# Two transformer blocks on one Trainium2 core: the start is reordered, and three visits of four modulation slabs move to layer boundaries

## Reference

```python
# first block, for layer L in 0, 1
h = rms_norm(x, norm_w[L])
q, k, v, z, q_h, f_h, i_h, g_h, gate_a, gate_h = split(h @ w_in[L])
a = window_attention(rope(q, positions), rope(k, positions), v, sinks[L]) * silu(z)
b = norm(hgrn2(silu(q_h), f_h, i_h)) * silu(g_h)      # gated linear recurrence
x = x + (sigmoid(gate_a) * (a @ w_up_attn[L]) + sigmoid(gate_h) * (b @ w_up_hgrn[L])) @ w_out[L]
x = rms_norm(x, final_norm_w)
# second block, for layer i in 0, 1
mod = silu(c) @ ada_w[i] + ada_b[i]                   # ada_w[i] is 1024 x 6144; 6 vectors of 1024
sh_t, sc_t, g_t, sh_c, sc_c, g_c = split(mod, 6)
y = mixer_i(x * (1 + sc_t) + sh_t, rel_bias)          # i = 0: top-k latent attention; i = 1: differential
x = layer_norm(alpha * x + (1 + g_t) * y)
y = square(relu((x * (1 + sc_c) + sh_c) @ w1[i])) @ w2[i]
x = layer_norm(alpha * x + (1 + g_c) * y)
```

## Time and profile before

| | us |
|---|---|
| three executions without the profiler | 1336.64, 1339.19, 1339.91 (median 1339.19) |
| the profiled execution, its own time | 1346.1 |
| its span, first to last instruction | 1344.0 |
| PE busy in it | 1131.1 (84%) |
| POOL, ACT, DVE busy | 743.7, 550.8, 483.0 |
| mean granted clock of TensorE | 0.893 |

### The profile page before, as it was taken

The page is one execution under the profiler, slowest core; times in us unless marked ns, Lnnn a source line. Parts: engine busy times, 40 slices in busy tenths (PEclk is TensorE's granted clock), DMA queues, the critical chain, the costliest instruction groups (busy, mean ns, idle before and its releaser), DMA issues.

```text
span 1344.0 us, 15901 instructions
## 1 busy us (share of the span) xinstructions
PE 1131.1 (84%) x6584; PEld 954.6 (71%) x6584; DVE 483.0 (36%) x689; ACT 550.8 (41%) x749; POOL 743.7 (55%) x341
## 2 busy tenths in 40 slices
PE   2789698787796988879889699999698657999995
PEld 0778576656685766669678698888687446899894
DVE  3426633232457152323752511113600564301114
ACT  2455354323544363344442344344224432444441
POOL 1475362744464554646204487778457206588883
PEclk9899899897897988989857899999799668899997
DMA  7365333745461535475302366775287203456550
GB/s 282 119 248 190 128 124 114 243 176 178 177 238 65 188 105 208 147 245 157 126 0 66 99 230 231 278 261 180 92 302 272 88 0 126 153 181 195 175 174 32
DMA packets 101022, 221.58 MB, mean 165 GB/s; under 512 B 11360, under 2 KB 17878, under 8 KB 94806
## 3 DMA queue, kind: packets, MB, share of 16 engines
q1 hardware_dynamic: 95776, 210.29, 45.9%
q10 hardware_dynamic: 5174, 10.28, 2.1%
HBM read 219.48 MB, written 1.07 MB: 164 GB/s over the span
## 4 chain that ended last, share of the span: by engine, by line
PE 67%; DVE 14%; ACT 7%; DMA 4%; issue 3%; POOL 3%; ACTq 1%; POOLq 0%; DVEq 0%; SPq 0%
PE lin_ps L321 12%; PE lin_ps L322 11%; PE lin_ps L323 11%; PE tmp_ps L328 5%; PE tmp_ps L330 5%; PE tmp_ps L329 5%; PE tmp_ps L376 3%; PE lin_ps L328 3%; POOL wlo L805 3%; PE tmp_ps L419 2%; PE lin_ps L329 2%; PE lin_ps L330 2%; PE tmp_ps L516 2%; DMA ring<-in_b_w_in 2%; ACT whi L880 2%
## 5 line engine op out<-in xcount | busy, mean ns | idle before, releaser
L805 POOL TENSOR_TENSOR wlo<-ring,whi 128x1024 fp32r<-128x1024 f32 (+2 forms) x304 | 724.6, 2396 | 484.3 <-ACT whi L880 483.3
L880 ACT CAST whi<-ring 128x1024 fp32r<-128x1024 f32 (+2 forms) x304 | 312.6, 1035 | 534.2 <-PE lin_ps L323 244.2
L321 PE MATMUL lin_ps<-whi,hThi 128*128 128x512 f32 (+2 forms) x528 | 212.3, 402 | 27.2 <-POOL wlo L805 12.1
L322 PE MATMUL lin_ps<-wlo,hThi 128*128 128x512 f32 (+2 forms) x528 | 206.3, 391 | 0.0
L323 PE MATMUL lin_ps<-whi,hTlo 128*128 128x512 f32 (+2 forms) x528 | 205.9, 390 | 0.0
L328 PE MATMUL tmp_ps<-hThi,whi 128*128 128x256 f32 x520 | 149.5, 287 | 4.9 <-DVE hTlo L1517 4.9
L330 PE MATMUL tmp_ps<-hThi,wlo 128*128 128x256 f32 x520 | 148.7, 286 | 0.0
L329 PE MATMUL tmp_ps<-hTlo,whi 128*128 128x256 f32 x520 | 148.7, 286 | 0.0
L321 PEld LDWEIGHTS lin_ps<-whi,hThi 128*128 128x128 f32 x528 | 103.4, 196 | 60.1 <-issue 20.8
L328 PE MATMUL lin_ps<-hThi,whi 128*128 128x256 f32 x352 | 106.8, 303 | 30.2 <-POOL wlo L805 18.1
L323 PEld LDWEIGHTS lin_ps<-whi,hTlo 128*128 128x128 f32 x528 | 102.8, 195 | 20.8
(11 more groups left out here) (246 smaller groups left out, 1514.2 us busy)
## 6 DMA issues: line engine op xcount, KB each, us to landing
ring<-in_mlp_w SPq DMA_DIRECT2D x64, 1024.0 KB, 5.3
ring<-in_ada_w SPq DMA_DIRECT2D x48, 1024.0 KB, 5.5
ring<-in_w_in SPq DMA_DIRECT2D x40, 1024.0 KB, 5.3
ring<-in_b_w_in SPq DMA_DIRECT2D x12, 1024.0 KB, 5.7
ring<-in_w_out SPq DMA_DIRECT2D x8, 1024.0 KB, 5.2
ring<-in_a_w_in SPq DMA_DIRECT2D x6, 1024.0 KB, 5.8
ring<-in_w_up_hgrn SPq DMA_DIRECT2D x4, 1024.0 KB, 6.1
ring<-in_w_up_attn SPq DMA_DIRECT2D x4, 1024.0 KB, 9.8
```

The lines of the kernel that those rows point to most:

```text
L321: pe.matmul(ps, xh, hi, start=first, stop=False, skip_group_check=True)
L322: pe.matmul(ps, xh, lo, start=False, stop=False, skip_group_check=True)
L805: pool.tensor_tensor(wlo[:, n % PARTS, :, 0:width], ring[:, u % RING, 2 * h:2 * h + 2, 0:width], whi[:, n % PARTS, :, 0:width].bitcast(F32 ...
L880: act.copy(whi[:, n % PARTS, :, 0:width], ring[:, u % RING, 2 * h:2 * h + 2, 0:width]).then_inc(S("high_formed"), 1)
```

## The change

Nothing is computed otherwise; the order changes.

- **Start.** Layer 0 of the first block has no visit before its first product. On ACT, the squares of x come right after the issue of the transfers, then the first three highs, and only then what needs `cols`. On DVE the scaling of x comes first, then `cols`, the turned operand's low part, and after it the angles, `lbw` and `lams`. PE does `relvec` after the `kv` product, before the visit there. `csil`, the two bias loads (`gate_bias`, 512 KB each) and the Sin stand on ACT behind the Silu of `qh`. SP waits for x before it loads the second weight block. `posi` has a semaphore of its own. POOL waits for the scaled x before it forms the first lows (`f_scaled`, in both layers).
- **Visits.** The visits of 4 at the start of layer 0 and before `aT` in both layers go. Visits of 4 come at the boundaries `s0`, `s1` and `s2`, on PE before the wait for x, on DVE after the scaled x. Layer 1's visit of 4 stays. So group 0 fills at the end of layer 0 (and closes there, without the spread row), group 1 at layer 1's level 6, group 2 at `s0`, where it is closed after `s0iq`.

The diff, cut to its core (the long DVE block is moved as it is):

```diff
+ADA_BOUNDARIES = ("s0", "s1", "s2")
...
-            pe.wait_ge(S("small_landed"), 16 * 10)
+            pe.wait_ge(S("small_landed"), 16 * 9)
             ps = open_tmp("cols")
             pe.transpose(ps[:, 0, 0:P], stackA[:], ident[:])
             close_tmp(pe.transpose(ps[:, 0, P:P + 5 + 8 * KT], stackB[:], ident[0:5 + 8 * KT, 0:5 + 8 * KT]), "cols")
-            ps = open_tmp("relvec")
-            pe.wait_ge(S("rel_landed"), 32)
-            close_tmp(pe.matmul(ps[0:16, 0, 0:DIST], relT[:], onehot[:], start=True, stop=True), "relvec")
             quads_a = [(i, g) for i in range(NT) for g in range(2)]
             for L in range(2):
                 w = I["w_in"][L]
-                if L == 0:
-                    pe.wait_ge(S("csil"), 1)
-                ada(4)
+                if L:
+                    ada(4)
                 pe.wait_ge(S("f_scaled"), L + 1)
                 feature_major(f"f{L}hT", hs)
...
                 linear_tok(f"f{L}kv", w, K0, 256, hT)
+                if L == 0:
+                    ps = open_tmp("relvec")
+                    pe.wait_ge(S("rel_landed"), 32)
+                    close_tmp(pe.matmul(ps[0:16, 0, 0:DIST], relT[:], onehot[:], start=True, stop=True), "relvec")
+                    pe.wait_ge(S("csil"), 1)
...
-                ada(4)
                 pe.wait_ge(S("f_a"), L + 1)
...
+                if name in ADA_BOUNDARIES:
+                    ada(4)
...
+            ada_close()
...
+                if n == 1:
+                    sp.wait_ge(S("x_landed"), 16)
                 if n >= RING:
...
             row, one = st[:, 1, :, 0], st[:, 2, :, 0]
             rstd("f0", row, one)
+            pool.wait_ge(S("f_scaled"), 1)
             rstd("f0h", st[:, 1], st[:, 2], "f0ho")
             rstd("f1", row, one, "f0out1")
+            pool.wait_ge(S("f_scaled"), 2)
             rstd("f1h", st[:, 1], st[:, 2], "f1ho")
...
             act.dma_start(posi[:], I["positions"].rearrange("b (i p) -> p (b i)", p=P),
-                          allow_slow_non_contiguous=True).then_inc(S("small_landed"), 16)
+                          allow_slow_non_contiguous=True).then_inc(S("posi_landed"), 16)
...
-            act.wait_ge(*read_of("cols"))
-            act.activation(csil[:], colA[:, 120:128].unsqueeze(2).broadcast_to([P, KT, ADA_ROWS]), ACT.Silu
-                           ).then_inc(S("csil"), 1)
-            act.wait_ge(S("angles"), 1)
-            act.activation(trig[:], ang[:], ACT.Sin).then_inc(S("trig"), 1)
-            act.wait_ge(S("lb_max"), 1)
-            act.activation(lbw[:, 0:2, :], lbw[:, 0:2, :], ACT.Exp).then_inc(S("lb_exp"), 1)
-            act.wait_ge(S("lam_dots"), 1)
-            act.activation(lams[:, 0:2], lams[:, 0:2], ACT.Exp).then_inc(S("lam_exp"), 1)
-            act.wait_ge(*read_of("relvec"))
-            act.dma_start(scratch, relvec).then_inc(S("scratch_written"), 16)
                 if L == 0:
-                    for j in range(2):
-                        gate_bias(0, j)
                     squares("f0", (S("x_landed"), 16))
+                    high_parts(PARTS, 0)
+                    act.wait_ge(*read_of("cols"))
...
+                if L == 0:
+                    act.wait_ge(S("lb_max"), 1)
+                    act.activation(lbw[:, 0:2, :], lbw[:, 0:2, :], ACT.Exp).then_inc(S("lb_exp"), 1)
+                    act.wait_ge(S("lam_dots"), 1)
+                    act.activation(lams[:, 0:2], lams[:, 0:2], ACT.Exp).then_inc(S("lam_exp"), 1)
                 ahead(f"f{L}f")
...
                 read(act.activation(flat(qin), flat(ps), ACT.Silu), f"f{L}qh")
+                if L == 0:
+                    act.activation(csil[:], colA[:, 120:128].unsqueeze(2).broadcast_to([P, KT, ADA_ROWS]), ACT.Silu
+                                   ).then_inc(S("csil"), 1)
+                    for j in range(2):
+                        gate_bias(0, j)
+                    act.wait_ge(S("angles"), 1)
+                    act.activation(trig[:], ang[:], ACT.Sin).then_inc(S("trig"), 1)
...
                 read(act.mul(qkv[:, :, 0:HALF], ps, HD ** -0.5), f"f{L}q")
+                if L == 0:
+                    act.wait_ge(*read_of("relvec"))
+                    act.dma_start(scratch, relvec).then_inc(S("scratch_written"), 16)
...
-            ps = full_tmp_of(dve, "cols")
-            dve.tensor_copy(colA[:], ps[:, 0, 0:P])
-            read(dve.tensor_copy(colB[:], ps[:, 0, P:P + 5 + 8 * KT]), "cols")
-            ps = full_tmp_of(dve, "relvec")
-            read(dve.tensor_copy(relvec, ps[0:16, 0, 0:DIST]), "relvec")
-            dve.wait_ge(S("small_landed"), 16 * 10)
...
-                ada()
+                if L:
+                    ada()
+                else:
+                    ps = full_tmp_of(dve, "cols")
+                    dve.tensor_copy(colA[:], ps[:, 0, 0:P])
+                    read(dve.tensor_copy(colB[:], ps[:, 0, P:P + 5 + 8 * KT]), "cols")
                 for h in range(2):
...
+                if L == 0:
+                    dve.wait_ge(S("posi_landed"), 16)
+                    dve.wait_ge(S("invf"), 1)
+                    step(dve.tensor_copy(posf[:], posi[:]))
+                    for i in range(NT):
...
+                if L == 0:
+                    ps = full_tmp_of(dve, "relvec")
+                    read(dve.tensor_copy(relvec, ps[0:16, 0, 0:DIST]), "relvec")
                 ada()
...
-                ada()
                 low_of(f"f{L}aT0", 0)
...
+            ada()
...
+                if after in ADA_BOUNDARIES:
+                    ada()
                 if n == 3:
...
+            ada_close()
```

More of the change, by code:

```diff
@@ L1180, in _ @@
                               ).then_inc(S("levels_both"), 1)
-            ps = full_tmp_of(dve, "cols")
-            dve.tensor_copy(colA[:], ps[:, 0, 0:P])
-            read(dve.tensor_copy(colB[:], ps[:, 0, P:P + 5 + 8 * KT]), "cols")
-            ps = full_tmp_of(dve, "relvec")
-            read(dve.tensor_copy(relvec, ps[0:16, 0, 0:DIST]), "relvec")
-            dve.wait_ge(S("small_landed"), 16 * 10)
-            dve.wait_ge(S("invf"), 1)
-            step(dve.tensor_copy(posf[:], posi[:]))
@@ L1191, in _ @@
-            for i in range(NT):
-                for c in range(2):
-                    ins = dve.tensor_scalar(ang[:, i, c, :], invf[:], posf[:, i:i + 1], None, ALU.mult)
-            step(ins)
-            for c in range(2):
-                ins = dve.tensor_scalar(angk[:, :, c, :], ang[:, :, c, :], 1.0 / TURN, 0.25 * c, ALU.mult, ALU.add)
-            step(ins)
-            step(dve.tensor_scalar(angk[:], angk[:], ROUNDER, None, ALU.add))
-            step(dve.tensor_scalar(angk[:], angk[:], -ROUNDER, None, ALU.add))
@@ L1200, in _ @@
-            for part in TURN_PARTS:
-                step(dve.scalar_tensor_tensor(ang[:], angk[:], -part, ang[:], ALU.mult, ALU.add))
-            step(dve.tensor_scalar(ang[:, :, 1, :], ang[:, :, 1, :], TURN / 4, None, ALU.add))
-            dve.tensor_scalar(ang[:], ang[:], SIN_MAX, -SIN_MAX, ALU.min, ALU.max).then_inc(S("angles"), 1)
-            step(dve.tensor_copy(lbw[:, 0:2, :], colA[:, 16:24].rearrange("p (l h) -> p l h", l=2)))
-            step(dve.tensor_tensor(lbw[:, 2, :], lbw[:, 0, :], lbw[:, 1, :], ALU.max))
@@ L1207, in _ @@
-            dve.tensor_tensor(lbw[:, 0:2, :], lbw[:, 0:2, :], lbw[:, 2, :].unsqueeze(1).broadcast_to([P, 2, 4]),
-                              ALU.subtract).then_inc(S("lb_max"), 1)
-            dve.wait_ge(S("lb_exp"), 1)
-            step(dve.tensor_tensor(lbw[:, 2, :], lbw[:, 0, :], lbw[:, 1, :], ALU.add))
-            step(dve.reciprocal(lbw[:, 2, :], lbw[:, 2, :]))
-            step(dve.tensor_tensor(lbw[:, 0:2, :], lbw[:, 0:2, :], lbw[:, 2, :].unsqueeze(1).broadcast_to([P, 2, 4]),
-                                   ALU.mult))
@@ L1214, in _ @@
-            step(dve.tensor_tensor(lbw[:, 3, :], lbw[:, 0, :], lbw[:, 1, :], ALU.add))
-            step(dve.tensor_tensor(lbw[:, 3, :], lbw[:, 3, :], lbw[:, 0, :], ALU.subtract))
-            step(dve.tensor_scalar(lbw[:, 4, :], lbw[:, 3, :], -1.0, 1.0, ALU.mult, ALU.add))
-            dve.wait_ge(S("lamb_landed"), 16)
-            for n in range(2):
-                step(dve.tensor_tensor(lamb[:, 2 * n, :], lamb[:, 2 * n, :], lamb[:, 2 * n + 1, :], ALU.mult))
-                ins = dve.tensor_reduce(lams[:, n:n + 1], lamb[:, 2 * n, :], AX.X, ALU.add)
@@ L1222, in _ @@
-            ins.then_inc(S("lam_dots"), 1)
-            dve.wait_ge(S("lam_exp"), 1)
-            step(dve.tensor_tensor(lams[:, 2:3], lams[:, 1:2], lams[:, 0:1], ALU.subtract))
-            step(dve.tensor_scalar(lams[:, 3:4], lams[:, 2:3], -LAM_INIT, None, ALU.add))
-            step(dve.tensor_scalar(lams[:, 4:5], colB[:, 2:3], 1.0 - LAM_INIT, None, ALU.mult))
             visited, folded = [0], [0]
```

33 lines of the change are left out of this document (added).

## The result

The changed kernel takes 1306.96 us (median of four runs, 1303.27 to 1310.16); the kernel before, measured beside it, 1339.55 (1336.64 to 1342.23). The ratio is 0.9756, with a 95% interval of 0.9717 to 0.9796: 32.6 us faster. The prediction was 1301.0 in a range of 1290 to 1315.

A forecast was written before the change was run, and what follows sets the result against it. PE's work plus its gaps bound the kernel (PE busy 84% of the span). Terms summed to -38.2 us: profiled 1346.1 becomes 1307.9, and the median, 6.9 lower, 1301.0; range 1290 to 1315.

The forecast's parts named there:

- the closing behind `s0iq`: Closing group 2 after `s0iq` takes 1.7 us, filling a 2.15-us wait of PE for ACT: 0.
- The sign of being wrong that the prediction named: At four places, the second weight block lands 9.1 us after the first's issue; otherwise the forecast is wrong.
- The start: Layer 0's first product starts 24.2 us earlier, at 19.3; after payback -20.6 us, bounds -16.9 to -24.
- the payback: At the start, paid back: 0.8 for the fourth half, 1.9 for `csil`, two issues and Sin, 0.9 for `relvec`.
- In the new order SP holds back all blocks but one: At the start, about 2 MB share the DMA engines instead of 5, so x lands at 8 us.
- The removed visit gives nothing of itself: At the start, the removed visit stood in PE's wait for x, so its removal alone gives nothing.
- Level 6: Layer 0: group 0 no longer fills here, so the visit doesn't wait 3.40 for DVE: -5.5 us, bounds -4.5, -6.3.
- Before `aT` in layer 0: Without the visit's slabs, `w_up_hgrn` is loaded early and PE's 5.33 wait for a low goes: -6.0 us, bounds -4 to -8.
- Layer 1's boundary: The visit starts earlier, so the next weights are issued earlier and PE starts at 311.25: -6.5 us, bounds -4, -8.
- `s0`: New visit at this boundary; weights and bias table share DMA, second block lands at +12: +4.0 us, bounds 0 to +7.
- `s1` and `s2`: New visits at these boundaries, weights last, DVE loses 0.9 to a low: +1.3 and +1.1 us, bounds -2.3 to +3.5 each.
- The step from profile to median: The median lies 6.9 us under the profiled execution, before and after: 1307.9 profiled gives 1301.0.

The follow-up runs named there:

- the three edits together: Changed kernel with the `s0` visit back before `aT` in layer 1, no SP wait for x, third low held back: 1299.02 us, ratio 0.9683.

## Why the prediction held, and where it was off

**The mechanism was right at most places, and the closeness of the sum is in part luck.** The prediction speaks of nine places; its sum has eight terms (the ninth, the closing behind `s0iq`, was put at 0). Every term but one came out within 1.6 us, and the sum was 4.5 us too large (38.2 against 33.7). With the kernel's own medians, 32.6 apart, the difference is 5.6, which is what 1301.0 is off by (1306.96, less the 0.4 that the kernel before's median rose).

**The sign of being wrong that the prediction named did come.** It said that the forecast is wrong if the second block lands at another time than 9.1 us after the first's issue. It was ready 8.0 us after it at layer 1's boundary, 8.2 at `s1`, 8.0 at `s2` and 13.7 at `s0`; at the start it took 8.4 from its own issue, where I had 5 to 6. So it isn't one duration that four places share; at `s0` the run with the later table shows 8.6. The total stayed near because the errors went both ways: the landing was forecast 1 us too late at three places, and about 3 too early at `s0` (+12 against +14.7) and at the start.

**The start.** -20.6 against -20.9 is luck, two errors that cancel. The second block was issued at 8.13, as forecast, and taken to allow a third high that ends at 15; with two more blocks issued right behind it, it landed for a high that ended at 17.62, and the product came 1.6 later than forecast. On the other side the payback was 1.7 and not 3.6: PE waits 0.24 for the fourth half where I had 0.8, and the 1.9 for `csil`, two issues and the Sin became 0.1 (PE's wait of 1.06, forecast at about 3): the issues ran beside ACT's table load.

**"In the new order SP holds back all blocks but one"** was the wrong reason for an early x. The run without that wait shows x landing as early, 7.2 us after its issue beside four weight blocks. What differs from the kernel before (10.4 beside four slabs) is that weights and not slabs stand beside x; beside one slab, in the run with the start's visit, it was 7.7. The rows of a slab in memory are 8 KB long, those of a weight block 2 KB and those of x 4 KB. The Trainium skill (DMA: Bandwidth & Descriptors, Queues, rings and completion order) says that an engine of the DMA takes turns between queues by the packet. By it a queue with smaller pieces leaves x a greater share, which would fit; no run here changed the rows alone.

**"The removed visit gives nothing of itself"** fits the rows of the old order only, where the visit was over at 26.97 and the three highs at 34.19, both before x was scaled at 38.05 (no run takes the visit alone out of the old order). With the squares early, the visit's slabs would have held the ring: of the 22.6 us, 13.0 come with the new order alone (43.51 to 30.50) and 9.6 when the visit goes too. The sum contained both, since it let the weights be first in the ring; the sentence gave it all to x.

**Level 6** held (-6.05 for -5.5): the run with the start's visit closes the group there again and loses 5.6 across it (its distance to the changed kernel grows from 10.65 to 16.3).

**Before `aT` in layer 0**, -4.4 and not -6.0: the bound that I named, ACT's earlier highs holding up the attention's last copy, took 0.95, and PE then waits 2.88 for `f_a`.

**Layer 1's boundary** went as forecast and gave 7.7 where I had 6.5, at the edge of the bounds, since the second block came 1.1 us sooner; this is read from the rows, no run takes the place by itself.

**`s0`** is the term that was mis-sized: +6.9 and not +4.0. That the table and the weights share the engines was in it, and the run with the later table shows 5 us for this. The 1.6 MB and 390 GB/s gave the second block at +12; it came at about +14.7, of which the runs show the table's part (+9.7 without it) but not how the two queues divided the engines.

**`s1` and `s2`** came out right (+1.3, +1.0), again by two errors that cancel: the third high ended at +10.3 where I had +11.4, and DVE's stop cost 2.0 where I had 0.9. The forecast said that the weights are last; the run with the third low held back shows that without DVE's stop the visit would cost `s1` and `s2` nothing (+14.1 and +14.0, against +14.9 and +15.1 before the change). So the rule of exclusion that I put in a sentence by itself deserved a place in the sum.

**The step from profile to median.** I took the profiled execution to stay 6.9 above the median. It was 6.9 above in the kernel before, whose attention in `s0` had a clock of 0.52, and 3.7 below in the changed one, at 0.78. The sum of the places against the medians would have been the better base.

## What to carry to other kernels

A filler of PE's time that is loaded through the same ring as the weights costs at a boundary what it takes of the ring, not what it takes of PE: taking it out of the start, where it held back the first weights, gave 9.6 us at the first product, and of the moves to the boundaries the one to `s0` lost 1.4 net by its two places. What else such a move shifts (here a group's closing, 6 to 8 us at level 6 and 1.6 behind `kv`) can be worth more than the move. Before a second transfer is put beside a burst of weights, ask which of them is wanted first; 2 MB issued 0.25 us behind the first weights, and not after the operand, cost 5 us at `s0`. And where two engines exclude each other, a semaphore that holds back the one with slack can be worth more than an earlier start of the other: at `s1` it gave 2 us at its place, and the earlier start of ACT gave none. That the gains at these places reach the total is shown only for the three edits together.

## What the runs showed of the hardware

- A cast on DVE, SBUF to SBUF, took 2.47 us beside a low of POOL and 0.69 without; the low part 3.24 and 1.23; the scaling of x in two parts 5.63 and 1.42. The Trainium skill (SBUF — State Buffer, Who interferes with whom) says that a cast in a two-port mode excludes GpSimd for the whole instruction. The trace agrees, which the earlier trace rows could not yet show for the cast: it ends 0.55 us after the low that began 0.4 before it.
- Two instructions on ACT that issue transfers stand in the program behind the Silu of `qh` and its table load, and ran at 53.44 and 54.15, the table load at 53.98 and the Silu at 55.27.
- The second weight block of a burst was ready for ACT 8.0 us after the first's issue at layer 1's boundary, 8.2 at `s1`, 8.6 at `s0` without the table and 13.7 with it. That is +9.2 at `s1` from the last product's end. The estimate by the fit of the Trainium skill (DMA: Bandwidth & Descriptors, Anatomy of one DMA), 4.4 us for a block, would be +6.5; no boundary came near it. That section gives the fit for a single transfer on GpSimd's path, and these are several of SP's, one behind the other.
- The granted clock of an unchanged stage was 0.52, 0.60, 0.70 and 0.78 in four executions of two kernels, and the stage took 53.0, 50.4, 47.2 and 45.9 us.
